# Differential attention: half of the stacking transfers issued by ScalarE, and three identity products an item

## The reference, cut to what matters

```python
def diff_attend(q1, q2, k1, k2, v, lam):
    scale = DIFF_QK_DIM ** -0.5
    s1 = jnp.einsum('bqhd,bkhd->bhqk', q1, k1).astype(jnp.float32) * scale
    s2 = jnp.einsum('bqhd,bkhd->bhqk', q2, k2).astype(jnp.float32) * scale
    p = jax.nn.softmax(s1, axis=-1) - lam * jax.nn.softmax(s2, axis=-1)
    return jnp.einsum('bhqk,bkhd->bqhd', p.astype(v.dtype), v)
```

## Time and profile before

| what | value |
|---|---|
| median of three runs | 3149.83 us (3145.11 to 3153.69) |
| profiled execution, its own time | 3149.23 us |
| span of its trace | 3147.6 us |
| mean granted TensorE clock | 0.965 |
| busy: TensorE, VectorE, ScalarE | 94%, 54%, 32% of the span |
| DMA mean rate | 101 GB/s |

### The profile page before, as it was taken

One profiled execution on the slowest core, in us unless ns is written; L12 is line 12 of the kernel. 1 busy time (PEld: TensorE's weight loads), 2 busy tenths in 40 slices (PEclk: granted clock), 3 DMA queues, 4 the chain that ended last, 5 costly groups with the idle time before them and its releaser, 6 DMA issues.

```text
span 3147.6 us, 39340 instructions
## 1 busy us (share of the span) xinstructions
PE 2967.3 (94%) x15639; PEld 2495.1 (79%) x15639; DVE 1690.8 (54%) x2220; ACT 1007.0 (32%) x1389; POOL 106.5 (3%) x150
## 2 busy tenths in 40 slices
PE   7999999999989999899878999999999977989998
PEld 5888887978868888589667778888887957768886
DVE  5655655444456765564575455555545157454454
ACT  3333333232333222322355232112214235332222
POOL 0000000000001100000000000000000000000000
PEclk8999999999999999999879999999999988999999
DMA  6343444534234544232510212333222150222331
GB/s 231 111 131 100 137 149 154 166 104 152 71 120 141 169 123 131 87 94 81 136 39 14 82 47 81 95 100 95 88 67 74 41 134 29 66 67 82 99 100 67
DMA packets 269422, 318.97 MB, mean 101 GB/s; under 512 B 25259, under 2 KB 236603, under 8 KB 269276
## 3 DMA queue, kind: packets, MB, share of 16 engines
q1 hardware_dynamic: 243100, 232.83, 24.1%
q0 software_dynamic: 19456, 72.00, 7.5%
q10 hardware_dynamic: 6720, 12.06, 1.2%
HBM read 294.05 MB, written 11.27 MB: 97 GB/s over the span
## 4 chain that ended last, share of the span: by engine, by line
PE 85%; DVE 5%; DVEq 3%; ACT 2%; SPq 2%; issue 1%; DMA 1%; ACTq 0%
PE psum L573 25%; PE psum L574 24%; PE psum L575 24%; PE psum L897 3%; SPq L531 2%; PE psum L651 2%; PE psum L907 1%; PE psum L680 1%; PE psum L726 1%; DVE n_t L1559 1%; ACT pt L1442 1%; DMA ada<-in_w_ada 1%; PE psum L794 1%; DVEq L1558 1%; PE psum L713 1%
## 5 line engine op out<-in xcount | busy, mean ns | idle before, releaser
L1571 DVE TENSOR_TENSOR w_lo<-raw,w_hi 128x2048 fp32r<-128x2048 f32 (+1 forms) x244 | 435.2, 1784 | 467.8 <-ACT w_hi L1081 360.8
L573 PE MATMUL psum<-hs_hi,w_hi 128*128 128x512 f32 x1632 | 648.0, 397 | 36.5 <-DVE hs_lo L1563 27.7
L574 PE MATMUL psum<-hs_hi,w_lo 128*128 128x512 f32 x1632 | 639.9, 392 | 0.0
L575 PE MATMUL psum<-hs_lo,w_hi 128*128 128x512 f32 x1632 | 639.7, 392 | 0.0
L573 PEld LDWEIGHTS psum<-hs_hi,w_hi 128*128 128x128 f32 x1632 | 309.3, 190 | 109.5 <-issue 36.5
L575 PEld LDWEIGHTS psum<-hs_lo,w_hi 128*128 128x128 f32 x1632 | 309.1, 189 | 65.8
L574 PEld LDWEIGHTS psum<-hs_hi,w_lo 128*128 128x128 f32 x1632 | 309.5, 190 | 63.1 <-issue 1.0
L1626 DVE SCALAR_TENSOR_TENSOR ada_acc<-ada_raw,csil,ada_acc 128x512 f32<-128x512 f32 x392 | 279.8, 749 | 44.4 <-DMA ada_raw<-in_w_ada 25.4
L573 PE MATMUL psum<-mid_hi,w_hi 128*128 128x512 f32 x768 | 299.3, 390 | 0.0
L574 PE MATMUL psum<-mid_hi,w_lo 128*128 128x512 f32 x768 | 299.1, 389 | 0.0
L575 PE MATMUL psum<-mid_lo,w_hi 128*128 128x512 f32 x768 | 298.8, 389 | 0.0
(11 more groups left out here) (320 smaller groups left out, 4632.6 us busy)
## 6 DMA issues: line engine op xcount, KB each, us to landing
raw<-in_w_in SPq DMA_DIRECT2D x56, 1024.0 KB, 5.2
ada_raw<-in_ada_w POOLq DMA_DIRECT2D x96, 512.0 KB, 4.3
raw<-in_w_ff SPq DMA_DIRECT2D x48, 1024.0 KB, 5.5
raw<-in_w_ff SPq DMA_DIRECT2D x96, 512.0 KB, 3.4
ada_raw<-in_w_ada POOLq DMA_DIRECT2D x32, 512.0 KB, 4.6
raw<-in_w_in SPq DMA_DIRECT2D x24, 512.0 KB, 5.1
ada<-in_w_ada SPq DMA_DIRECT2D x4, 2048.0 KB, 18.6
raw<-in_w_ret_out SPq DMA_DIRECT2D x16, 512.0 KB, 3.4
```

What stands on the lines that cost most here:

```text
L573: pe.matmul(dst, lhi, rhi, start=start, stop=False)
L574: pe.matmul(dst, llo, rhi, start=False, stop=False)
L575: return pe.matmul(dst, lhi, rlo, start=False, stop=stop)
L1571: dve.tensor_tensor(w_lo[par][:, 0:kt], raw[par][:, 0:kt], w_hi[par][:, 0:kt].bitcast(F32), ALU.subtract).then_inc(lo_done, 1)
```

## The change

Two things change. First, the 24 DMAs of a layer that read partitions 64 to 127 (`a = 1`, `stacked[1]`) are issued by ScalarE; SP issues only those of `a = 0`, and those of `qcs` as before. ScalarE's 24 stand in three pieces between its copies. Second, TensorE computes three products of `ident` by `ident` into `T2` between the values of item i - 1 and the transposes of item i; nobody reads them. That is 23 times in the first layer and 15 in the second, 114 products.

```diff
+        STACKS = ((ks, 0, S, dfk_hi, (0, 1)), (ks, 0, S, dfk_lo, (2, 3)), (qs, 0, S, dfq_hi, (0, 2)), (qs, 0, S, dfq_lo, (1, 3)),
+                  (ks, S, SC, dfkc_hi, (0, 1)), (ks, S, SC, dfkc_lo, (2, 3)))
...
                 sp.wait_ge(df_split, 4 * l + 3)
-                for a in range(2):
-                    for half in range(2):
-                        stack(ks, 0, S, dfk_hi, (0, 1), a, half, stacked[a])
-                        stack(ks, 0, S, dfk_lo, (2, 3), a, half, stacked[a])
-                        stack(qs, 0, S, dfq_hi, (0, 2), a, half, stacked[a])
-                        stack(qs, 0, S, dfq_lo, (1, 3), a, half, stacked[a])
-                        stack(ks, S, SC, dfkc_hi, (0, 1), a, half, stacked[a])
-                        stack(ks, S, SC, dfkc_lo, (2, 3), a, half, stacked[a])
+                for half in range(2):
+                    for operand, c0, w, part, quads in STACKS:
+                        for q in quads:
+                            sp.dma_start(operand[32 * q:32 * q + 32, half:8:4, c0:c0 + w].bitcast(F32),
+                                         part[32 * half:32 * half + 32].bitcast(F32)).then_inc(stacked[0], 16)
...
+            def keep_busy(count):
+
+                for _ in range(count):
+                    pe.matmul(T2[:, 0:P], ident[:], ident[:], start=True, stop=True)
+
             def attention(l, kind, sems, score, values):
...
                         mm.then_inc(pv, 1)
+                        if kind == "diff" and i < len(its):
+                            keep_busy(3)
                     if i < len(its):
                         it = its[i]
...
+                def stack_odd(half, ks_):
+
+                    for operand, c0, w, part, quads in ks_:
+                        for q in quads:
+                            act.dma_start(operand[32 * q:32 * q + 32, 2 + half:8:4, c0:c0 + w].bitcast(F32),
+                                          part[64 + 32 * half:96 + 32 * half].bitcast(F32)).then_inc(stacked[1], 16)
+
+                act.wait_ge(df_split, 4 * l + 3)
+                stack_odd(0, STACKS[0:4])
                 for c in range(2):
                     act.wait_ge(f2_done, 3 * l + c + 1)
                     act.copy(y_fo[:, c, :], (X0, X1)[c][:]).then_inc(f2_read, 1)
+                    if c == 0:
+                        stack_odd(0, STACKS[4:6])
                 if wc:
                     act.wait_ge(f2_done, 3)
                     act.mul(y_foc[:], C0[:].rearrange("p (c s) -> p c s", c=2), 2.0 ** 0.5).then_inc(f2_read, 1)
+                stack_odd(1, STACKS)
```

More of the change, by code:

```diff
@@ L526, in _ @@
                 sp.dma_start(na_mask[:], d["na_mask"]).then_inc(ln_in, 16)
-                def stack(dst, c0, w, src, quads, a, half, landed):
-                    r0, t0 = 64 * a + 32 * half, 2 * a + half
-                    for q in quads:
-                        sp.dma_start(dst[32 * q:32 * q + 32, t0:8:4, c0:c0 + w].bitcast(F32),
-                                     src[r0:r0 + 32].bitcast(F32)).then_inc(landed, 16)
-                sp.wait_ge(df_split, 4 * l + 3)
-                for a in range(2):
-                    for half in range(2):
-                        stack(ks, 0, S, dfk_hi, (0, 1), a, half, stacked[a])
-                        stack(ks, 0, S, dfk_lo, (2, 3), a, half, stacked[a])
-                        stack(qs, 0, S, dfq_hi, (0, 2), a, half, stacked[a])
-                        stack(qs, 0, S, dfq_lo, (1, 3), a, half, stacked[a])
-                        stack(ks, S, SC, dfkc_hi, (0, 1), a, half, stacked[a])
-                        stack(ks, S, SC, dfkc_lo, (2, 3), a, half, stacked[a])
+                sp.wait_ge(df_split, 4 * l + 3)
+                for half in range(2):
[3 more added lines that the diff above has]
+                                         part[32 * half:32 * half + 32].bitcast(F32)).then_inc(stacked[0], 16)
                 if l == 0:
                     sp.wait_ge(df_split, 4)
-                    for a in range(2):
-                        for half in range(2):
-                            stack(qcs, 0, SC, dfqc_hi, (0, 2), a, half, stacked_c)
-                            stack(qcs, 0, SC, dfqc_lo, (1, 3), a, half, stacked_c)
+                    for t0 in range(4):
+                        for part, quads in ((dfqc_hi, (0, 2)), (dfqc_lo, (1, 3))):
+                            for q in quads:
+                                sp.dma_start(qcs[32 * q:32 * q + 32, t0:8:4, :].bitcast(F32),
+                                             part[32 * t0:32 * t0 + 32].bitcast(F32)).then_inc(stacked_c, 16)
                 sp.wait_ge(sg_out, 3 if l == 0 else 5)
```

## The result

The changed kernel takes 3156.09 us (median of 20 runs, 3151.38 to 3160.31) against 3149.53 us for the kernel before on the same chip (20 runs, 3143.64 to 3157.57): ratio 1.0022 [1.0016, 1.0028]. It is 0.2% slower. The forecast of 3146 us had the sign wrong; the range held the time.

The account below looks back on a forecast made before the run. TensorE was taken as busy nearly everywhere, with only the two differential attention stretches able to move. The sum was 3149.2 - 12.6 + 2 x 4.5 = 3145.6, said as 3146 us, practically no change; range 3136 to 3158.

Parts of the forecast that it names:

- x: How much later the last DMA of `stacked[0]` lands in each layer, delaying first scores; taken as 4.5 us.
- upper end of 7.3: Bound on the later landing if a packet takes as long with two queues: 22.7 us of all engines' time.
- the forecast case: Clock held and landing 1.6 to 7.3 us later: 3139.8 to 3151.2 us, chance 0.50.
- The meeting on the write side: Both queues write partitions 0 to 63, then 64 to 127, and would meet there: a delay between the two bounds.
- The stage: Differential attention, first scores to end of last values: -8.3 us first layer, -4.3 second, together -12.6 us.
- the clock that the products hold: Fillers fill idle gaps, so the clock, once up, stays up to the stage's end, context items included.
- Rival 3: Fillers do not hold the clock and are pure cost: 3171 to 3180 us; chance 0.08.
- ScalarE's issues: 24 DMAs at 0.64 us fill ScalarE's idle time, done by 1543.5, with 1.8 us to spare before the exponentials.
- Rival 4: Issues on ScalarE cost 0.8 us or more, first exponentials slip 2 to 4 us a layer: about 3151; chance 0.07.
- Rival 1: The queues do not disturb each other, landing under 1.6 us later: 3136.6 to 3139.8 us; chance 0.26.
- Rival 2: Two queues slow each other in issuing too, up to 1.2 us each, landing up to 15 us later; chance 0.09.

Follow-up runs that it names:

- e4_swap: Changed kernel with ScalarE's DMAs in swapped pairs, writing the other partition quarters than SP in each step; 3152.36 us, ratio 1.0003 to the kernel before.
- e2_act: Changed kernel without the identity products, only the division of DMAs between SP and ScalarE left; 3155.24 us, ratio 1.0013 to the kernel before.
- e9_tail: Kernel before, but ScalarE issues the last 8 of 48 DMAs, once the 18th of `stacked[0]` has landed; no identity products; 3142.24 us, ratio 0.9983.
- e16_pad2: Kernel before with 24 unread identity products ahead of TensorE's wait for `stacked[0]` in the second layer; 3150.25 us, ratio 1.0002.
- e1_fillers: Kernel before with only the three identity products an item added, all transfers by SP as before; 3148.51 us, ratio 0.9992.
- e5_quarter: Changed kernel, but ScalarE issues only 12 of its 24 DMAs; SP issues the other 12 behind `stacked[0]`; 3148.42 us, ratio 0.9988 to the kernel before.
- e3_split: Changed kernel with both queues carrying `stacked[0]` first (SP half 0, ScalarE half 1), then `stacked[1]`; 3154.99 us, ratio 1.0011 to the kernel before.
- e6_source: Changed kernel, but ScalarE's 24 DMAs read partitions 0 to 63, as SP's do, instead of 64 to 127; 3167.71 us, ratio 1.0059 to the kernel before.

## Why the prediction was wrong

**x, the later landing.** This is the step that failed: 4.5 us a layer was taken, 7.5 and 8.3 were measured, past even the upper end of 7.3. In the sum that is 15.8 instead of 9.0, +6.8 us. The forecast was 3.6 us below the profiled execution before, and 8.0 above it were measured; of these 11.6 us x is 6.8, the stage 1.3, the first layer behind it 5.4, and the rest -1.9. The mechanism of x was the one of the forecast case; the size was chosen between the bounds, with the 358 GB/s of another kind of transfer as the lower one. That rate had no bearing. The row of this very kind, share 0.89 at 203 GB/s, was the right one: 203 / 0.89 = 228 GB/s, which is the 229 measured, and 5.24 MB at that rate are 23 us. The upper bound, which comes from this row, was 0.2 and 1.0 us short and should have been the value.

**The meeting on the write side** (the Trainium skill, "SBUF — State Buffer", "Door 1: The DMA port swizzle") hardly shows: e4_swap has x = 7.2 and 7.1, against 7.5 and 8.3. On the read side there is something of it: 192 to 198 GB/s where both queues read partitions 0 to 63, below the page's 218 and below the 229 with sources on both halves.

**The stage.** -12.6 us was forecast, -11.3 measured, and place by place it is within 1.0 us: to item 4 -2.4 in the first layer (forecast -2.4), -2.9 in the second (-2.3); items 4 to 13 +2.3 and +2.6 (+1.9 and +2.2), with 3.82 us an ordinary item (1567.64 - 1563.82; 3.9); behind item 13 -6.8 and -4.0 (-7.8 and -4.2).

**But the credit was wrong.** The forecast gave the stage's gain to the clock that the products hold. They did hold it in the stage, in every trace that has three in every item. But e2_act has as short a stage without them, at the low clock from 1620 us on, and e9_tail nearly so: what the clock gave, the products took. The DMA half alone has both stages together 14.3 us shorter than before, the products alone 4.7, the two together 11.3. Without head 1's wait the low stretches also lie elsewhere (1620 instead of 1604 us in e2_act); how much of the 14.3 is the wait and how much the clock, no run separates. And the sum stopped at the stage's end: the 5.4 us of longer time behind it, with the clock at 0.87 over it against 0.91 before, had no term. That they are the products' doing is not shown: e2_act has 88.2 us there without them, e4_swap 84.2 with them, and e16_pad2 89.0 with the first layer's program of before. e1_fillers prices the half at 0.9992 [0.9982, 1.0002], some 2.5 us and not told from zero, where 7 to 10 us were my expectation. Rival 3, that the clock would fall as before despite them, is refuted. What was said for it was misread as well: in the 44.3 us at the low clock TensorE did not always have work, it was busy 33.28 of them.

**ScalarE's issues** went nearly as said: most at 0.64 us, the first at up to 0.83, done at 1543.8 (forecast 1543.5), the table load behind them, no exponential late. Rival 4 did not occur. Rival 1 (x below 1.6) is refuted by every kernel in which ScalarE issued DMAs of `stacked[1]` from the start (2.2 us at least, e5_quarter). Rival 2 was not this kernel's, but the mechanism exists (e3_split, and e6_source with x = 11.5). SP's issues slowed little, 16.4 us for 24 against 15.5.

What stays open: why the clock falls near 1606 us in some executions and not in others of nearly the same order of work, and so how much of a difference of 2 us between two of these kernels is the edit's.

## What to carry to other kernels

When a second queue takes over transfers, add the bytes that will be under way before the one that is waited for, and divide by the rate at full share that this kind of transfer shows (rate by share, here 203 / 0.89). Move only what is needed late, and start it late: 8 of 48 DMAs issued behind the critical ones gained 0.17%, 24 issued beside them lost 0.13% (0.22% with the products). Before a gain or loss of a few tenths of a per cent is put down to an edit, look for TensorE waits "issue" at the turns of loops in both traces, since adding or removing instructions ahead of a loop can be worth as much by itself (0.19% here), and follow the clock past the end of the stage that was edited, in more than one execution.

## What was unexpected in the hardware

- The rate of SBUF to SBUF DMAs of 32 partitions from two queues: 229 GB/s with sources on both halves of the partitions, 192 to 198 with all on one half; the half written to first makes 1.2 us of difference at most (first scores after 24.3 and 24.1 us against 24.5 and 25.4).
- The price of issuing a DMA is not fixed: 0.64 us, but up to 1.4 us on both queues when both read the same 64 partitions (2.54 to 2.75 us a pair).
- A turn of a loop can stall TensorE by 1.6 to 2.2 us, with low clock of some 3 us behind it, or not at all, by 23 products more ahead of it: 6.6 us for two turns. With 69 more it is there.
